# A recurrent mixer on one core: the heads' values projected token-major in four units, centred by row means, and three convolution units moved between the heads

## The chip, the cores and the metric

The kernel runs on one core of one Trainium2 chip. The metric is the time of one execution on the device in microseconds (us). The core has five engines that run side by side and meet through semaphores: TensorE (PE; its weight loads are shown as PEld), VectorE (DVE), ScalarE (ACT), GpSimd (POOL) and SyncE (SP), which here only issues DMAs.

## The reference

A network over 512 tokens of width 1024, all in float32. It starts with two layers (`DEPTH = 2`) that have a mixer between two feed-forward parts. Only these two mixers are touched; what follows them (attention, memory, a linear recurrence) is not:

```python
p = rmsnorm(x, mix_norm) @ w_in          # 512 + 768 + 2048 columns
y_a = gmlp_mixer(p[:, :512])             # gelu, group layer norm, 128x128 token mixing
y_b = shortconv_mixer(p[:, 512:1280])    # bg, cg, xin: bg * conv3(cg * xin)
y_c = retention_mixer(p[:, 1280:])       # 4 heads of 128: q, k, v, gate
x = x + concat(y_a, y_b, y_c) @ w_out

# retention, per head and chunk of 128 tokens
q, k = rotary(q), rotary(k) * 128 ** -0.5
scores = (q @ k.T) * decay
inner = scores @ v
kv = (k * zeta).T @ v                    # the state that a chunk hands on
state = state * gamma + kv
ret = inner + (q @ previous_state) * xi
ret = layernorm_over_the_head(ret) * gn
y_c = silu(g) * ret
```

The layer norm takes the mean over the 128 values of a head away. Since `ret` is linear in `v`, the kernel takes the mean out of `v` at once and only divides by the root of the variance at the end.

## The kernel before, in words

Activations lie with features on partitions and the 512 tokens along the columns. A weight matrix comes as a stream of units of 128 x 1024 float32 (eight blocks of 128 x 128, one for each 128 input features). There are 588 units and four slots. For each unit SP loads `raw`, ACT rounds it to fp32r (`whi`, in `split_hi`, called as `ahead(key)` two units ahead), POOL subtracts to get the rest (`wlo`), and PE makes 24 matmuls of 512 columns: `whi` by the high and by the low part of the activations, `wlo` by the high part. `project` does a whole unit; `high` and `low` do its first 16 and its last 8, so that something can stand between them. Four PSUM banks go round (`next_bank`); 4 to 7 are claimed by name. The order on every engine is written out by hand.

The mixer (`mixer1`, once in each engine's program) goes through 26 units. Units 0 to 3 feed the gated part (gelu, group means and variances). Then come four heads of four units each:

* unit 4+4h gives v with features on partitions; DVE multiplies it by the token scale R into `vT`. After two more units, `vturn` multiplies each 128-token block of `vT` by the matrix `centring` (identity less 1/128): that turns it to tokens on partitions and takes the head mean away in one go. ACT copies it to `vtok`.
* units 5+4h and 6+4h give k and q; DVE rotates each with four operations (`rotate`), into `kr` and `qr`.
* unit 7+4h gives the gate. Between its `high` and `low` PE turns `kr` (`kturn`), and after it come `kv1`, `score1`, the products with the states, and `inner`.
* PE takes the variance of head h-1 (`head_variance`) after the first unit of head h. DVE then does `finish_head(h-1)`: a reciprocal, two products and `split`, which writes the high and the low part of y tile 4+h-1.

DVE also has the two `gate_norm` (a reciprocal and a product each) at the ends of heads 0 and 1. After the heads PE turns the gated values, runs unit 20, `head_variance(3)`, the token mixing (`gmix`), then units 21 to 25 for the two convolution tiles, and then `output`. DVE goes through `conv_gate(0)`, `gmlp(0)`, `gmlp(1)`, `conv(0)`, `finish_head(3)`, `conv_gate(1)`, `conv(1)`. `output` multiplies by w_out with the y tiles in the order

```python
Y_ORDER = (4, 5, 6, 0, 1, 7, 2, 3)
for m in range(X_EARLY):     # 3 output tiles, the first six y tiles of each
    part((kind, a, m), banks[m][:, :], pairs, range(0, 6), True, False, arrive if m == 0 else None)
```

so that in the first output tile PE waits for each y tile just before it uses it: tiles 4, 5, 6 (heads 0 to 2), 0 and 1 (the gated part), 7 (head 3), and, after 54 matmuls, 2 and 3 (the convolutions).

Of the kernel before, what the change touches and what calls it, by code (L numbers as in the profile page):

```python
# [6 lines left out]
F32 = mybir.dt.float32  # L7
# [6 lines left out]
P = 128  # L14
# [30 lines left out]

F_STAGE = (0, 2, 3, 5, 8, 11)
# [31 lines left out]
def unit_order():  # L78
# [8 lines left out]
    def mixer1(l):  # L87
        out.extend(("m1", l, n) for n in range(26))
        out.extend(("o1", l, m) for m in range(KD))
# [29 lines left out]
def low_part(u):  # L119
# [5 lines left out]
    "m1_vector": "ga ws rot_table gelu_lo csq_lo centred centring z0 vinv vn hinv ret_n ret_g y1h y1 rot_c rot_s rot_in rope vT gg sm "  # L125
                 "sg ret qx state rsq_lo gbias gm cg cg2 z cv cvR cy",
    "m1_scalar": "gelu gelu_hi csq csq_hi vroot hroot vtok ktok silu1 rsq rsq_hi vtg",
    "m1_tensor": "mean var hvar vturn kturn kv1 score1 inner gturn gmix",
# [40 lines left out]
class Memory:  # L169
# [51 lines left out]
    def mixer1_tiles(self, l):  # L221
        return self.scoped(f"m1{l}", [
            ("yh", KD * SEQ, F32R), ("yl", KD * SEQ, F32R), ("ct", SEQ, F32), ("sn", SEQ, F32),
            ("dk", 2 * C_HEADS * P + C_HEADS, F32), ("below_qx", 5 * P - C_HEADS, F32), ("qx", 3 * P, F32), ("ws", 4 * P, F32), ("bs", 2 * P, F32), ("kr", SEQ, F32), ("qr", SEQ, F32),
            ("t1", SEQ, F32), ("vT", SEQ, F32), ("vtok", SEQ, F32), ("sm", SEQ, F32),
            ("ktok", 3 * P, F32), ("state", 3 * P, F32), ("ret", SEQ, F32),
            ("rsq", SEQ, F32), ("inv", SEQ, F32), ("sg", SEQ, F32), ("centring", P, F32), ("ga", SEQ, F32),
# [96 lines left out]
def tensor_program(pe, S, M):  # L324
# [156 lines left out]
    def mixer1(l):  # L481
# [35 lines left out]
        for h in range(C_HEADS):  # L517
            b = next_bank("vT", l, h)
            high(("m1", l, 4 + 4 * h), b[:, :])
            if h == 0:  # L520
                gate_variances()
            low(("m1", l, 4 + 4 * h), b[:, :])
            if h:
                head_variance(h - 1)
            project(("m1", l, 5 + 4 * h), next_bank("rot_in", l, h, 0)[:, :])
            project(("m1", l, 6 + 4 * h), next_bank("rot_in", l, h, 1)[:, :])
            b4 = claim(4, "vtok", l, h)
            pe.wait_ge(*S.at("vT", l, h))
# [13 lines left out]
            pe.wait_ge(*S.at("vtok", l, h))  # L542
# [2129 lines left out]
```

## Time and profile before

| | |
|---|---|
| median of 3 runs | 3239.8 us (3239.62 to 3239.84) |
| the profiled execution | 3240.1 us, its span in the trace 3238.8 us |
| PE busy | 3227.0 us, 14914 matmuls |
| DVE, POOL, ACT busy | 1592.7, 1331.1 and 1090.2 us |
| granted clock of TensorE | full over the span |
| HBM read | 316 MB, 98 GB/s over the span |

The span is what the trace covers; the execution's own time is a little longer. An engine's busy time is the union of its instructions. A line of the profile can be that of a helper: L363, L364 and L367 are `unit`, L378 and L379 `high`, L385 `low`.

### The profile page before, as it was taken

What the parts mean: (1) busy time and instruction counts of PE and PEld (TensorE: products, weight loads), DVE (VectorE), ACT (ScalarE), POOL (GpSimd) and SP (SyncE); (2) the same over time, 40 slices, a digit from 0 to 9 for tenths busy, and PEclk for the clock granted to TensorE, in tenths of its full rate; (3) what the DMA queues carried; (4) which work ended last, traced back from release to release, by engine and by line L of the source; (5) the groups of instructions that cost most, each with busy time, mean ns of one, the idle gap of its engine ahead of it and who ended that gap; (6) DMA issues with size and microseconds to landing.
All of it is one profiled execution on the core that took longest, in us unless ns stands there. A gap on an engine that the chain in (4) does not pass through costs nothing.

```text
span 3238.8 us, 36579 instructions
## 1 busy us (share of the span) xinstructions
PE 3227.0 (100%) x14914; PEld 2678.1 (83%) x14914; DVE 1592.7 (49%) x1845; ACT 1090.2 (34%) x1449; POOL 1331.1 (41%) x551
## 2 busy tenths in 40 slices
PE   9999999999999999999999999999999999999999
PEld 7888888888888888888888877888888888988887
DVE  6441277554234531676544267545444486454421
ACT  4222332322232222433222345543222475432222
POOL 4444433544444445334444432224444213154443
PEclk9999999999999999999999999999999999999999
DMA  4223322322232223322323322323222223232222
GB/s 151 98 98 104 116 72 81 108 98 98 98 111 93 99 95 104 106 82 91 104 92 101 104 92 66 124 92 104 98 98 101 98 92 136 92 104 98 98 94 82
DMA packets 92182, 321.57 MB, mean 99 GB/s; under 512 B 10480, under 2 KB 12912, under 8 KB 92016
## 3 DMA queue, kind: packets, MB, share of 16 engines
q1 hardware_dynamic: 86624, 311.54, 28.9%
q10 hardware_dynamic: 5392, 7.69, 0.7%
q8 instruction: 119, 1.95, 0.3%
q14 instruction: 47, 0.39, 0.0%
HBM read 316.05 MB, written 2.10 MB: 98 GB/s over the span
## 4 chain that ended last, share of the span: by engine, by line
PE 99%; DVE 1%; DMA 0%; ACT 0%; issue 0%; ACTq 0%; DVEq 0%
PE bank L363 20%; PE bank L367 20%; PE bank L364 20%; PE bank L378 9%; PE bank L385 9%; PE bank L379 9%; PE bank L348 1%; PE bank L349 1%; PE bank L352 1%; PE bank L642 1%; PE bank L662 1%; PE bank L767 0%; PE bank L762 0%; PE bank L761 0%; PE bank L394 0%; PE bank L395 0%
## 5 line engine op out<-in xcount | busy, mean ns | idle before, releaser
L2488 POOL TENSOR_TENSOR wlo<-raw,whi 128x1024 fp32r<-128x1024 f32 x535 | 1326.5, 2489 | 1886.1 <-ACT whi L950 1885.6
L950 ACT ACTIVATE whi<-raw 128x1024 fp32r<-128x1024 f32 x588 | 611.8, 1052 | 594.6 <-PE bank L385 382.0
L363 PE MATMUL bank<-gxh,whi 128*128 128x512 f32 x1552 | 606.2, 391 | 0.0
L364 PE MATMUL bank<-gxl,whi 128*128 128x512 f32 x1552 | 604.1, 389 | 0.0
L378 PE MATMUL bank<-gxh,whi 128*128 128x512 f32 x1296 | 507.0, 391 | 2.2 <-ACT whi L950 2.2
L379 PE MATMUL bank<-gxl,whi 128*128 128x512 f32 x1296 | 504.4, 389 | 0.0
L363 PE MATMUL bank<-f_hh,whi 128*128 128x512 f32 x1056 | 410.8, 389 | 0.0
L364 PE MATMUL bank<-f_hl,whi 128*128 128x512 f32 x1056 | 410.8, 389 | 0.0
L367 PE MATMUL bank<-gxh,wlo 128*128 128x512 f32 x1552 | 383.6, 389 | 0.0
L1760 DVE TENSOR_TENSOR f_u<-bank,R 128x512 f32<-128x512 f32 x132 | 91.2, 691 | 583.0 <-PE bank L385 583.0
L1705 DVE SCALAR_TENSOR_TENSOR x<-bank,x 128x512 f32<-128x512 f32 x96 | 66.4, 692 | 565.1 <-PE bank L367 539.2
L363 PEld LDWEIGHTS bank<-gxh,whi 128*128 128x128 f32 x1552 | 291.3, 188 | 61.8 <-issue 0.7
L367 PEld LDWEIGHTS bank<-gxh,wlo 128*128 128x128 f32 x1552 | 291.2, 188 | 60.9 <-DVE wlo L1666 0.4
L364 PEld LDWEIGHTS bank<-gxl,whi 128*128 128x128 f32 x1552 | 291.3, 188 | 60.7 <-issue 0.7
L385 PE MATMUL bank<-gxh,wlo 128*128 128x512 f32 x1296 | 322.8, 391 | 0.0
L1765 DVE TENSOR_SCALAR f_hh<-f_u 128x512 fp32r<-128x512 f32 x132 | 312.1, 2364 | 4.5
L1024 ACT ACTIVATE f_s<-f_a 128x512 f32<-128x512 f32 x132 | 83.4, 632 | 638.6 <-DVE f_a L1756 638.6
L378 PEld LDWEIGHTS bank<-gxh,whi 128*128 128x128 f32 x1296 | 243.3, 188 | 54.6 <-issue 2.3
L385 PEld LDWEIGHTS bank<-gxh,wlo 128*128 128x128 f32 x1296 | 242.5, 188 | 51.1 <-issue 1.0
L379 PEld LDWEIGHTS bank<-gxl,whi 128*128 128x128 f32 x1296 | 243.3, 188 | 49.6
L367 PE MATMUL bank<-f_hh,wlo 128*128 128x512 f32 x1056 | 262.7, 389 | 0.0
L988 ACT ACTIVATE sq<-x 128x512 f32<-128x512 f32 x96 | 60.6, 632 | 573.2 <-DVE x L1705 573.2
(406 smaller groups left out, 3564.6 us busy)
## 6 DMA issues: line engine op xcount, KB each, us to landing
raw<-stream SPq DMA_DIRECT2D x588, 512.0 KB, 3.3
xa_mem<-memT ACTq DMA_DIRECT2D x2, 1024.0 KB, 6.1
m_dk<-decay ACTq DMA_DIRECT2D x2, 514.0 KB, 4.4
x<-xT ACTq DMA_DIRECT2D x4, 256.0 KB, 5.7
x<-xT SPq DMA_DIRECT2D x4, 256.0 KB, 6.9
outT<-x ACTq DMA_DIRECT2D x4, 256.0 KB, 2.2
outT<-x SPq DMA_DIRECT2D x4, 256.0 KB, 2.6
m_ct<-cos ACTq DMA_DIRECT2D x2, 256.0 KB, 2.7
```

Of the source, the lines that this page charges most:

```text
L363: pe.matmul(out, seq(hi, k, P), h, start=first and k == 0, stop=False)
L364: pe.matmul(out, seq(hi, k, P), l, start=False, stop=False)
L367: mm = pe.matmul(out, seq(lo, k, P), h, start=False, stop=last and k == len(pairs) - 1)
L378: pe.matmul(out, seq(hi, k, P), gx[k][0], start=k == 0, stop=False)
L379: pe.matmul(out, seq(hi, k, P), gx[k][1], start=False, stop=False)
L385: mm = pe.matmul(out, seq(lo, k, P), gx[k][0], start=False, stop=k == KD - 1)
L950: act.activation(M.whi[r][:, :], M.raw[r][:, :], ACT.Copy).then_inc(*S.tick("hi", u))
L1024: act.activation(T["s"][:, :], T["a"][:, :], ACT.Silu).then_inc(*S.tick("silu", f, m))
L1705: dve.scalar_tensor_tensor(seq(M.x, m), at_bank("xs", i, m)[:, :], scale, seq(M.x, m), ALU.mult, ALU.add).then_inc(*S.tick("xs", i, m))
L1760: dve.tensor_tensor(T["u"][:, :], at_bank("u", f, m)[:, :], M.R[:, :], ALU.mult).then_inc(*S.tick("u", f, m))
L1765: dve.tensor_scalar(seq(T["hh"], m), T["u"][:, :], 1.0, None, ALU.mult).then_inc(*S.tick("hh", f, m))
L2488: pool.tensor_tensor(M.wlo[r][:, :], M.raw[r][:, :], M.whi[r][:, :].bitcast(F32), ALU.subtract).then_inc(*S.tick("lo", u))
```

## The change

* The values of all four heads come first, in four units of their own, ("m1v", l, 0) to ("m1v", l, 3). A unit holds two blocks of input features (k) by all 512 value columns. The 128-token blocks of the activations are now the stationary operand and the weight's 512 columns the moving one, so the result has tokens on partitions: bank n holds tokens 128n to 128n+127 of all four heads. Four ring banks are open over all four units.
* `norm` stands in the second of these units. Behind it `column_sums` makes the per-token sums of squares as a column (4 float32 matmuls of one column); ACT takes the root, DVE the reciprocal.
* For each bank DVE sums each head's 128 columns (`reduce_sum`) and makes the bias, minus mean times token scale; ACT writes `vtok` with four activations of 128 x 128 with scale and bias. The products of the heads read their block of `vtok`.
* Gone: the units 4, 8, 12 and 16 (their weights are in the new units), the DVE product into `vT`, the matrix `centring`, `vturn` and its 4 float32 matmuls a head, and the ACT copy a head.
* Units 20, 21 and 22 (the first convolution tile) move from behind the heads to the place where v stood in heads 1, 2 and 3. On DVE `conv_gate(0)`, `conv_sum(0)` and `conv_out(0)` stand there, ahead of `finish_head(h-1)`.
* The tables (`ct`, `sn`, `ws`) are scaled on DVE ahead of the row means; `gate_norm(0)` goes between the two rotations of head 0, `gate_norm(1)` to the end of head 0.
* Behind the heads PE has unit 23, `head_variance(3)`, `gmix`, units 24 and 25, `output`. DVE has `gmlp(0)`, `gmlp(1)`, `finish_head(3)`, `conv_gate(1)`, `conv_sum(1)`, `conv_out(1)`.

The core of the diff (`conv_sum` and `conv_out` are the two parts of the old `conv`, unchanged):

```diff
+M1_UNITS = (0, 1, 2, 3, 5, 6, 7, 20, 9, 10, 11, 21, 13, 14, 15, 22, 17, 18, 19, 23, 24, 25)
...
 tensor_program
+        def column_sums():
+            b = claim(6, "col_root", l)
+            pe.wait_ge(*S.at("acc", i - 1, KD - 1))
+            for n in range(NB):
+                mm = pe.matmul(b[:, n:n + 1], seq(M.acc, n, P), M.ones[:, 0:1], start=n == 0, stop=n == NB - 1)
+            mm.then_inc(*S.tick("colsum", l))
+
+        def token_values():
+            banks = []
+            for j in range(4):
+                u = U["m1v", l, j]
+                hi, lo = M.whi[u % SLOTS], M.wlo[u % SLOTS]
+                pe.wait_ge(*S.at("hi", u))
+                for blocks in ((0, 1), (2, 3)) if j == 3 else (range(NB),):
+                    for n in blocks:
+                        if j == 0:
+                            banks.append(next_bank("vtok", l, n))
+                        for k in (2 * j, 2 * j + 1):
+                            if n == 0:
+                                pe.wait_ge(*S.at("gx", i - 1, k))
+                            h, lw = (seq(t, k)[:, n * P:(n + 1) * P] for t in (M.gxh, M.gxl))
+                            pe.matmul(banks[n][:, :], h, seq(hi, k % 2), start=k == 0, stop=False)
+                            pe.matmul(banks[n][:, :], lw, seq(hi, k % 2), start=False, stop=False)
+                    if j == 1:
+                        norm(i)
+                        column_sums()
+                    pe.wait_ge(*S.at(*low_part(u)))
+                    for n in blocks:
+                        for k in (2 * j, 2 * j + 1):
+                            mm = pe.matmul(banks[n][:, :], seq(M.gxh, k)[:, n * P:(n + 1) * P], seq(lo, k % 2),
+                                           start=False, stop=k == KD - 1)
+                        if j == 3 and n < NB - 1:
+                            mm.then_inc(*S.tick("vdone", l, n))
+                mm.then_inc(*S.tick("used", u))
...
         for h in range(C_HEADS):
-            b = next_bank("vT", l, h)
-            high(("m1", l, 4 + 4 * h), b[:, :])
+            if h:
+                project(("m1", l, 19 + h), next_bank(("cg", "z", "cy")[h - 1], l, 0)[:, :])
+                head_variance(h - 1)
+            b = next_bank("rot_in", l, h, 0)
+            high(("m1", l, 5 + 4 * h), b[:, :])
             if h == 0:
                 gate_variances()
-            low(("m1", l, 4 + 4 * h), b[:, :])
-            if h:
-                head_variance(h - 1)
-            project(("m1", l, 5 + 4 * h), next_bank("rot_in", l, h, 0)[:, :])
+            low(("m1", l, 5 + 4 * h), b[:, :])
             project(("m1", l, 6 + 4 * h), next_bank("rot_in", l, h, 1)[:, :])
-            b4 = claim(4, "vtok", l, h)
-            pe.wait_ge(*S.at("vT", l, h))
-            pe.wait_ge(*S.at("centring", l))
-            for n in range(NB):
-                mm = pe.matmul(seq(b4, n, P), seq(T["vT"], n, P), T["centring"][:, :], start=True, stop=True)
-            mm.then_inc(*S.tick("vturn", l, h))
...
-        project(("m1", l, 20), next_bank("cg", l, 0)[:, :])
+        project(("m1", l, 23), next_bank("cg", l, 1)[:, :])
         head_variance(C_HEADS - 1)
...
-        for j in range(2):
-            if j:
-                project(("m1", l, 23), next_bank("cg", l, 1)[:, :])
-            project(("m1", l, 21 + 3 * j), next_bank("z", l, j)[:, :])
-            project(("m1", l, 22 + 3 * j), next_bank("cy", l, j)[:, :])
+        project(("m1", l, 24), next_bank("z", l, 1)[:, :])
+        project(("m1", l, 25), next_bank("cy", l, 1)[:, :])
...
 scalar_program
+        for n in range(NB):
+            act.wait_ge(*S.at("vbias", l, n))
+            for h in range(C_HEADS):
+                act.activation(seq(T["vtok"], n * C_HEADS + h, P), seq(bank[BANK["vtok", l, n]], h, P), ACT.Identity,
+                               bias=T["vcols"][:, 6 * NB + n * C_HEADS + h:6 * NB + n * C_HEADS + h + 1],
+                               scale=T["vcols"][:, NB + n:NB + n + 1]).then_inc(*S.tick("vtok", l, n))
...
             if h:
-                ahead(("m1", l, 4 + 4 * h))
+                ahead(("m1", l, 19 + h))
                 head_root(h - 1)
-            ahead(("m1", l, 5 + 4 * h))
+                ahead(("m1", l, 5 + 4 * h))
             ahead(("m1", l, 6 + 4 * h))
-            act.wait_ge(*S.at("vturn", l, h))
-            if h:
-                act.wait_ge(*S.at("inner", l, h - 1))
-            act.activation(T["vtok"][:, :], bank[4][:, :], ACT.Copy).then_inc(*S.tick("vtok", l, h))
             ahead(("m1", l, 7 + 4 * h))
...
 vector_program
+        for n in range(NB):
+            sums, bias = (T["vcols"][:, c + n * C_HEADS:c + (n + 1) * C_HEADS] for c in (2 * NB, 6 * NB))
+            dve.wait_ge(*(S.at("vdone", l, n) if n < NB - 1 else used("m1v", l, 3)))
+            dve.reduce_sum(sums, at_bank("vtok", l, n)[:, :].rearrange("p (h d) -> p h d", d=P), AX.X).then_inc(
+                *S.tick("vsum", l, n))
+            dve.wait_ge(*S.at("vsum", l, n))
+            dve.tensor_scalar(bias, sums, T["vcols"][:, NB + n:NB + n + 1], -1.0 / P, ALU.mult, ALU.mult).then_inc(
+                *S.tick("vbias", l, n))
...
         for h in range(C_HEADS):
-            dve.wait_ge(*used("m1", l, 4 + 4 * h))
             if h:
-                dve.wait_ge(*S.at("vturn", l, h - 1))
-            dve.tensor_tensor(T["vT"][:, :], at_bank("vT", l, h)[:, :], M.R[:, :], ALU.mult).then_inc(*S.tick("vT", l, h))
-            if h:
+                (conv_gate, conv_sum, conv_out)[h - 1](0)
                 finish_head(h - 1)
             rotate(h, 0, T["kr"])
+            if h == 0:
+                gate_norm(0)
             rotate(h, 1, T["qr"])
...
-            if h < 2:
-                gate_norm(h)
+            if h == 0:
+                gate_norm(1)
...
-        conv_gate(0)
         gmlp(0)
         gmlp(1)
-        conv(0)
         finish_head(C_HEADS - 1)
         conv_gate(1)
-        conv(1)
+        conv_sum(1)
+        conv_out(1)
```

## Rows read from the trace of the kernel before

**Rows 1.** The page: its span and first part (busy us, share, instructions)

```profile
span 3238.8 us, 36579 instructions
...
PE 3227.0 (100%) x14914; PEld 2678.1 (83%) x14914; DVE 1592.7 (49%) x1845; ACT 1090.2 (34%) x1449; POOL 1331.1 (41%) x551
```

**Rows 2.** Waits of PE: us in total, times, longest us

```profile
PE bank L378 <- ACT whi L950: 2.2, 1, 2.2
...
PE bank L458 <- DVE R L2461: 0.4, 1, 0.4
```

**Rows 3.** Timeline of PE, vturn of head 0: start us, us, engine, line

```profile
410.27 1.06 PE L531 MATMUL bank<-m_centring,m_vT 128*128 128x128 f32 x8
...
411.09 0.48 PE L378 MATMUL bank<-gxh,whi 128*128 128x512 f32 x1
...
411.40 0.39 PE L379 MATMUL bank<-gxl,whi 128*128 128x512 f32 x1
```

**Rows 4.** Timeline of PE, one-column float32 sums of another block

```profile
2037.02 0.95 PE L737 MATMUL bank<-ones,acc 128*128 128x1 f32 x8
2037.83 0.49 PE L363 MATMUL bank<-gxh,whi 128*128 128x512 f32 x1
```

**Rows 5.** Timeline of PE, from gmix to output, first mixer

```profile
508.72 2.57 PE L577 MATMUL bank<-m_ws,m_vtg 128*64 128x128 f32 x32
...
538.57 0.39 PE L348 MATMUL bank<-m_yh,whi 128*128 128x512 f32 x1
```

**Rows 6.** Timeline of DVE behind the heads, first mixer

```profile
511.06 2.32 DVE L1904 TENSOR_TENSOR m_ga<-m_ga,m_u 128x512 f32<-128x512 f32 x1
...
521.53 0.68 DVE L1921 TENSOR_TENSOR m_z<-bank,m_cg 128x512 f32<-128x512 f32 x1
...
522.77 1.54 DVE L1926 SCALAR_TENSOR_TENSOR m_cg<-m_z,lcol,m_cg 128x512 f32<-128x512 f32 x2
...
529.01 3.34 DVE L1827 RECIPROCAL m_inv<-m_inv 128x512 f32<-128x512 f32 x1
...
534.30 0.69 DVE L1777 TENSOR_TENSOR m_yl<-m_ret,m_yh 128x512 fp32r<-128x512 f32 x1
...
539.16 3.76 DVE L1926 SCALAR_TENSOR_TENSOR m_cg<-m_z,lcol,m_cg 128x512 f32<-128x512 f32 x2
```

**Rows 7.** Timeline of POOL, first mixer

```profile
428.24 4.76 POOL L2488 TENSOR_TENSOR wlo<-raw,whi 128x1024 fp32r<-128x1024 f32 x2 [1.79 <-ACT whi L950]
...
523.65 2.91 POOL L2488 TENSOR_TENSOR wlo<-raw,whi 128x1024 fp32r<-128x1024 f32 x1 [3.04 <-ACT whi L950]
...
539.97 2.40 POOL L2488 TENSOR_TENSOR wlo<-raw,whi 128x1024 fp32r<-128x1024 f32 x1 [2.72 <-ACT whi L950]
```

**Rows 8.** Timeline of PE in head 1: first matmul and kturn

```profile
420.42 0.48 PE L378 MATMUL bank<-gxh,whi 128*128 128x512 f32 x1
...
441.88 0.49 PE L538 MATMUL bank<-ident,m_kr 128*128 128x128 f32 x3
```

**Rows 9.** Timeline of DVE in head 1, and vT of head 3

```profile
427.71 0.68 DVE L1855 TENSOR_TENSOR m_vT<-bank,R 128x512 f32<-128x512 f32 x1
...
431.69 1.86 DVE L1829 TENSOR_TENSOR m_ret<-m_ret,m_inv 128x512 f32<-128x512 f32 x1
...
437.54 0.69 DVE L1848 TENSOR_TENSOR m_kr<-m_kr,m_t 128x512 f32<-128x512 f32 x1
...
480.40 0.69 DVE L1855 TENSOR_TENSOR m_vT<-bank,R 128x512 f32<-128x512 f32 x1 [2.44 <-PE bank L385]
```

**Rows 10.** Windows at the end: PE, PEld, DVE, ACT, POOL busy, PEclk, DMA

```profile
3231.50:3232.00 0.50, 0.40 (x1) 0.00 (x0) 0.50 (x2) 0.06 (x1) 0.00 (x0) 1.00 0.00 0
...
3236.00:3236.40 0.40, 0.00 (x0) 0.00 (x0) 0.00 (x0) 0.00 (x0) 0.00 (x0) 0.88 1.00 374
```

**Rows 11.** Groups by form: a reduction on DVE, the vtok copy on ACT

```profile
L2207 DVE TENSOR_REDUCE xa_mx<-bank 128x2 f32<-128x512 f32 x16 | 10.9, 683 | 5.1 <-PE bank L786 5.1
...
L1071 ACT ACTIVATE m_vtok<-bank 128x512 f32<-128x512 f32 x4 | 2.4, 600 | 38.6 <-PE bank L531 38.6
```

More of the change, by code:

```diff
@@ L87, in mixer1 @@
     def mixer1(l):
-        out.extend(("m1", l, n) for n in range(26))
+        out.extend(("m1v", l, j) for j in range(4))
+        out.extend(("m1", l, n) for n in M1_UNITS)
         out.extend(("o1", l, m) for m in range(KD))
@@ L558, in mixer1 @@
             for n in range(NB):
-                mm = pe.matmul(seq(b4, n, P), seq(T["vtok"], n, P), seq(T["sm"], n, P), start=False, stop=n == NB - 1)
+                mm = pe.matmul(seq(b4, n, P), seq(T["vtok"], n * C_HEADS + h, P), seq(T["sm"], n, P), start=False, stop=n == NB - 1)
             mm.then_inc(*S.tick("inner", l, h))
@@ L1032, in mixer1 @@
             act.dma_start(t[:, :], src).then_inc(*S.tick("tables", l, by=16))
[L1033 removed]
+        ahead(("m1v", l, 0))
+        ahead(("m1v", l, 1))
+        root(i)
+        act.wait_ge(*S.at("colsum", l))
+        act.activation(T["vcols"][:, 0:NB], bank[6][:, 0:NB], ACT.Sqrt, bias=EPS, scale=1.0 / D).then_inc(
+            *S.tick("col_root", l))
+        ahead(("m1v", l, 2))
+        ahead(("m1v", l, 3))
+        ahead(("m1", l, 0))
+        for n in range(NB):
[4 more added lines that the diff above has]
+                               scale=T["vcols"][:, NB + n:NB + n + 1]).then_inc(*S.tick("vtok", l, n))
         ahead(("m1", l, 1))
[L1035 removed]
         for j in range(4):
@@ L1515, in bank_plan @@
         residual(F_STAGE[2 * l])
+        for n in range(NB):
+            out["vtok", l, n] = ring.next()
         for j in range(4):
@@ L1518, in bank_plan @@
         for h in range(C_HEADS):
-            out["vT", l, h], out["rot_in", l, h, 0], out["rot_in", l, h, 1], out["gg", l, h] = ring.many(4)
-        for j in range(2):
-            out["cg", l, j], out["z", l, j], out["cy", l, j] = ring.many(3)
+            if h:
+                out[("cg", "z", "cy")[h - 1], l, 0] = ring.next()
+            out["rot_in", l, h, 0], out["rot_in", l, h, 1], out["gg", l, h] = ring.many(3)
+        out["cg", l, 1], out["z", l, 1], out["cy", l, 1] = ring.many(3)
         residual(M1_STAGE[l])
@@ L1848, in rotate, with gmlp @@
             dve.tensor_tensor(out[:, :], out[:, :], T["t1"][:, :], ALU.add).then_inc(*S.tick("rope", l, h, e))
+        def gmlp(j):
+            dve.wait_ge(*S.at("gmix", l, j))
+            bias = seq(T["bs"], j, P)[:, None, :].to_broadcast([P, NB, P])
+            dve.wait_ge(*S.at("silu1", l, C_HEADS - 1))
+            if j:
+                dve.wait_ge(*S.at("y1", l, j - 1))
+            dve.tensor_tensor(T["ga"][:, :].rearrange("p (n t) -> p n t", n=NB),
+                              bank[4 + j][:, :].rearrange("p (n t) -> p n t", n=NB), bias, ALU.add).then_inc(
+                *S.tick("gbias", l, j))
+            dve.wait_ge(*S.at("gbias", l, j))
+            dve.wait_ge(*S.at("gelu", l, 2 + j))
+            dve.tensor_tensor(T["ga"][:, :], T["ga"][:, :], seq(T["u"], j), ALU.mult).then_inc(*S.tick("gm", l, j))
+            dve.wait_ge(*S.at("gm", l, j))
+            split(T["ga"][:, :], j)
@@ L2563, in stream @@
             [10 + 12 + h for h in range(4)]
-        order = [2, 3, 0, 1]
-        order += [head[n][h] for h in range(4) for n in range(4)]
-        order += [6, 8, 4, 7, 9, 5]
+        of = [2, 3, 0, 1]
+        of += [head[n][h] for h in range(4) for n in range(4)]
+        of += [6, 8, 4, 7, 9, 5]
+        order = [of[n] for n in M1_UNITS]
+        v = i["w_in"][l][:, 18 * P:22 * P].reshape(4, 2, P, SEQ).transpose(0, 2, 1, 3).reshape(4, P, UNIT)
         wo = i["w_out"][l].reshape(KD, P, D)[list(Y_ORDER)].reshape(D, D)
-        out += [w[order], m_tiles(wo)]
+        out += [v, w[order], m_tiles(wo)]
         out += [pairs(i["ffn2_w_gate"][l], i["ffn2_w_up"][l]), tail_units(i["ffn2_w_down"][l])]
```

121 lines of the change are left out of this document (53 added, 68 removed).

## The prediction

> **What bounds the kernel now.** I read the page first: TensorE is busy for 3227.0 of 3238.8 us, and no other engine for half of the span [rows 1]. Then the waits of PE: three rows, the first and last of which are shown, with 3.7 us in all, and none of them in the two mixers [rows 2]. So the time is the sum of what PE issues. Less PE work shortens it one for one, and work taken off DVE, ACT or POOL gives nothing by itself. What can cost time is an order in which DVE, so far always early, comes late for PE. So I read the timelines of the mixer and laid the new order over them. The second mixer repeats the first; the rows shown are the first's.
>
> **What PE no longer does.** In `vturn` four float32 matmuls show as eight instructions. The first starts at 410.27 and the next matmul of the gate unit at 411.09, so they take 0.82 us; that next matmul itself takes 0.31 to the one behind it, where the usual pace is 0.23 [rows 3]. Without `vturn` a head is 0.90 us shorter; with 4 heads in 2 mixers this is **-7.2 us**. The number of units and of 512-column matmuls stays as it is: four new units of 24 stand for four old ones. Their operands change places, but each still loads 128 columns and streams 512. I take their pace as unchanged.
>
> **What PE does in addition.** `column_sums` has four float32 matmuls of one column. The same thing stands elsewhere in the kernel: 2037.02 to 2037.83, 0.81 us [rows 4], plus the same 0.09 at the change back. This is 0.9 us a mixer, **+1.8 us**.
>
> **The front, up to the gated units.** The four new banks go back to the ring for units 0 to 3, so the first `vtok` bank has to be read by the end of the fourth value unit. Its last matmul has 14 others behind it in that unit, 3.2 us. In that time DVE sums it (0.68 for 128x512, and I add 0.25 for the start and 0.1 for the bias), and ACT writes four blocks of 128x128. The nearest row is 0.60 us for 128x512 [rows 11], so four take 0.6 (by columns) to 2.4 (by instructions). I take 0.9, since most of the 0.60 goes with the columns. The sum is 1.9, and 0.6 more if the small DVE operation finds POOL at work, which I expect, since the third weight split of the stage comes then. That leaves 0.6 us: cost 0. With 2.4 for ACT and a whole POOL operation of 2.4 in front, it would be 2.6 us a mixer. The other edits here are free in the same way. The scaled tables fill a stretch in which DVE waits for the value units, and `gate_norm(0)` fits between the rotations of head 0: by my count its q is ready 0.7 us before the scores want it.
>
> **Behind the heads: the main cost.** `gmix` starts at 508.72 and takes 2.57; `output` starts at 538.57, five units later. That gives 27.28 us for 120 matmuls, 0.227 each, 5.45 a unit [rows 5]. Now only two units stand there, so `output` starts at 522.2 on the same scale. Ten matmuls later, at 524.5, it wants y tile 7, which `finish_head(3)` writes. On DVE, `gmlp(0)` and `gmlp(1)` take until 521.53, as in the trace [rows 6]: they start when `gmix` ends, and the weight splits of ACT and POOL beside them go by the same finished units in either kernel. `finish_head(3)` comes next: its reciprocal from 521.53 takes 3.34, and from its start to the end of its last operation the trace has 534.30 + 0.69 - 529.01 = 5.98 us [rows 6]. That alone gives 527.5. But POOL starts an operation at 523.65 [rows 7], and so it will again, as the split of the unit after next goes by the end of the second unit behind `gmix`. A DVE operation with both inputs in SBUF then waits for it: 511.06 shows 2.32 us for one that takes 0.69 free [rows 6]. `ret_n` asks at 524.9 and POOL is done at 526.0, so it ends at 526.6 and tile 7 is ready at 528.5. PE stands for 4.0 us, **+8.1 us** over both mixers. In the old order three more units, 16.4 us, covered this. Tile 3, the last one, is 6.8 us of DVE work behind, at 535.3, and wanted 54 matmuls and more after the stall, at 538.9, so there is no second wait. With no POOL operation in the way at all (5.9 us less in `gmlp`, 1.1 in `ret_n`) tile 7 would come at 521.5 and the wait would be 0: these are the ends, 0 and 8.1.
>
> The Trainium skill ("SBUF — State Buffer", section "Who interferes with whom") says that a DVE instruction with two SBUF inputs contends with a GpSimd instruction that reads SBUF, and that "Whoever issues first gets the shared pair for the whole instruction". The row at 511.06 agrees: 2.32 us in place of 0.69. By a reading in which they only share bandwidth, the wait behind the heads would be shorter.
>
> **The heads.** In head 1 the first matmul is at 420.42 and `kturn` at 441.88 [rows 8]. Without `vturn` PE wants the rotated k at 440.98. Before, it was ready at 438.23, 4.68 us after `ret_n` had ended at 433.55 [rows 9].
> Head 1: `conv_gate(0)` starts where `vT` did, 427.71 [rows 9]. Its second product asks at 428.4 and meets the POOL pair that starts at 428.24 with 2.38 each [rows 7]. It gets in after the first, 430.6, and is done at 431.2; POOL's second goes to 433.6. The reciprocal runs to 434.5. The next split used to wait on ACT behind `vturn`. Now it goes by unit 9, so POOL is at it from 433.6 to 436.0, `ret_n` ends at 436.6 and k is ready at 441.3: 0.35 us late, and 0.15 more because `qx` then holds up the states. In sum 0.5.
> Head 2, on the same scale: `conv_sum(0)` starts when its unit is done, at 426.2 (as `vT` does in head 3 [rows 9]). Its second sum would start at 428.20, POOL's pair at 428.24. Who wins is open. In the trace, with 0.11 us between them (523.54 and 523.65) DVE won, with 0.04 (539.93 and 539.97) POOL did and the pair of sums took 3.76 us in place of 1.54 [rows 6, 7]. If DVE wins, the products and the head's end fall behind two POOL operations and k is 0.8 late; if POOL wins, 1.85. With 0.15 for the states, 1.0 or 2.0; I take 1.5.
> Head 3: `conv_out(0)` is 1.8 us long, and k comes 0.5 us in time: 0.
> This makes 2.0 us a mixer, **+4.0 us**, with the ends 0 (POOL never in the way) and 5.0 (head 2 at 2.0, head 1 at 0.5) and a little more if head 3 slips.
>
> **Sum.** -7.2 + 1.8 + 0 + 8.1 + 4.0 = +6.7 us. The profiled execution took 3240.1 us, of which the span is 3238.8; the median shown is 0.3 lower. So 3240.1 + 6.7 - 0.3 = **3246.5 us**.
>
> **Rivals.**
> 1. *Not slower: the end of head 3 is in time.* This is one mechanism: POOL keeps out of `gmlp` and `ret_n`. It decides from 4.0 us earlier on. For it: with no POOL there, DVE needs 11.2 us from `gmlp(0)` on, and the cover is 14.2. Against it: the same blocks stand in both mixers of the trace. It gives 3246.5 - 8.1 = 3238.4.
> 2. *The heads hide everything.* DVE reaches `kturn` in time in all heads. For it: before, k was 3.6 us early in each. Against: my count of POOL operations. 3246.5 - 4.0 = 3242.5. With 1 and 2 together 3234.4, all of PE's saving; that would still be within 0.2%.
> 3. *The clock falls in the wait.* Full clock was still granted at 3232 us, where PE's last work ended, and it fell (from 2.4 towards 1.2 GHz) within 3236.0 to 3236.4, some 4.4 us later [rows 10]. My wait is 4.0 us long, just short of it. If it falls, matmuls at half the clock for about as long as the fall took, an estimate, cost 2.2 us each time: 3248.7 or 3250.9. The Trainium skill ("TensorE: Matmul & The Clock Gate", section "Why this matters for your kernels") warns that a long idle gap between bursts of matmuls takes the clock to its lower level. The rows at the end agree that it falls, and no run so far shows one inside the kernel.
> 4. *The front stalls*: up to 2.6 us a mixer, 3247 to 3252.
>
> **Chances.** My forecast with both outcomes of head 2 (3245.5 to 3247.5): 0.45. Rival 1: 0.1. Rival 2: 0.15, and both together 0.05. Rival 3: 0.15. Rival 4: 0.1. The range is 3240.5 to 3250.5: it leaves out rival 1 and the pair, and the far ends of 3 and 4. What a measurement of this kernel can tell from no change is about 0.2%, 6.5 us. The forecast sits on that bound (3246.3). Half of its own case, rivals 3 and 4 and a little of the rest lie above: slower 0.49, same 0.46. Faster by 6.5 us would need more than the 5.4 us that PE saves net, so it gets 0.05 for something I have not seen.
>
> **What would show it.** No L531 and about 64 fewer PE instructions for it, 16 more with one column. In the waits of PE's weight loads: two of some 4 us on `m_yl` at the first `output` unit, and four between 0.3 and 2 us at `kturn` in heads 1 and 2. The `vtok` copies should end before the fourth value unit does. If PE shows no wait at tile 7, my order of DVE and POOL behind the heads is wrong; if there are waits at unit 0 or in head 0, the front is.

## The result: 3251.9 us, 0.4% slower

| | before | after |
|---|---|---|
| median of 6 runs | 3239.82 us (3239.62 to 3240.08) | 3251.88 us (3251.15 to 3253.97) |
| ratio, 95% interval | | 1.0039 (1.0028 to 1.0049) |
| profiled execution, its span | 3240.1, 3238.8 us | 3251.4, 3248.8 us |

I forecast 3246.5 us, range 3240.5 to 3250.5. The direction was the likelier one of the forecast, the size is 5.4 us above it and outside the range. In the page of the changed kernel PE's busy time has not moved from [rows 1], and the span is 10.0 us longer:

```profile
span 3248.8 us, 36499 instructions
PE 3227.0 (99%) x14866; PEld 2675.3 (82%) x14866; DVE 1592.9 (49%) x1853; ACT 1098.0 (34%) x1475; POOL 1332.4 (41%) x551
```

48 instructions are gone, as forecast (64 of `vturn` less, 16 of the column sums more). The version without waits further down has the same matmuls and shows PE busy for 3222.5 us, so they were worth 4.5 us of busy time; that 3227.0 stands here again means that the remaining matmuls took as much longer, 3.4 of it at a lower clock (below). The waits of PE, to be read beside [rows 2], say where PE stood still (us in total, times, longest):

```profile
PE bank L351 <- DVE m_yl L1820: 8.0, 2, 4.1
PE bank L570 <- DVE m_kr L1897: 2.3, 2, 1.7
PE bank L381 <- ACT whi L979: 1.4, 1, 1.4
...
PE bank L582 <- DVE m_qr L1897: 0.4, 2, 0.2
```

L351 is the first tile of `output`, L570 `kturn`, L582 the scores. The timeline of PE at the first `output` unit of the first mixer, and a mixer later, answers to [rows 5]:

```profile
538.91 0.39 PE L352 MATMUL bank<-m_yl,whi 128*128 128x512 f32 x1
543.14 0.50 PE L351 MATMUL bank<-m_yh,whi 128*128 128x512 f32 x1 [3.85 <-DVE m_yl L1820]
...
1476.61 0.39 PE L352 MATMUL bank<-m_yl,whi 128*128 128x512 f32 x1
1481.12 0.50 PE L351 MATMUL bank<-m_yh,whi 128*128 128x512 f32 x1 [4.12 <-DVE m_yl L1820]
...
1484.55 0.63 PE L351 MATMUL bank<-m_yh,whi 128*128 128x512 f32 x1
1484.98 0.63 PE L352 MATMUL bank<-m_yl,whi 128*128 128x512 f32 x1
```

The tenth matmul starts at 538.91, the eleventh was due at 539.13 and comes at 543.14: 4.0 us late, and 4.3 in the second mixer. DVE behind the heads, beside [rows 6]:

```profile
524.96 0.69 DVE L1905 TENSOR_TENSOR m_ga<-bank,m_bs 128x512 f32<-128x512 f32 x1 [5.26 <-PE bank L609]
525.68 2.32 DVE L1910 TENSOR_TENSOR m_ga<-m_ga,m_u 128x512 f32<-128x512 f32 x1
...
536.15 3.35 DVE L1876 RECIPROCAL m_inv<-m_inv 128x512 f32<-128x512 f32 x1
539.53 1.64 DVE L1878 TENSOR_TENSOR m_ret<-m_ret,m_inv 128x512 f32<-128x512 f32 x1
...
542.39 0.69 DVE L1820 TENSOR_TENSOR m_yl<-m_ret,m_yh 128x512 fp32r<-128x512 f32 x1
543.00 0.68 DVE L1920 TENSOR_TENSOR m_cg<-bank,R 128x512 f32<-128x512 f32 x1
```

Tile 7 is ready when its `yl` ends, at 543.1, and PE goes on at 543.14. The last two PE rows above show what the forecast left to a rival: they start 0.43 us apart, and [rows 5] had 0.227. The windows of the first mixer (us, PE busy, then the granted clock, DMA share, GB/s):

```profile
542.00:543.00 1.00, 0.00 (x0) 1.00 0.88 315
543.00:544.00 1.00, 0.86 (x3) 0.82 0.35 139
544.00:545.00 1.00, 1.00 (x3) 0.50 0.00 0
...
546.00:547.00 1.00, 1.00 (x4) 0.50 0.00 0
547.00:548.00 1.00, 1.00 (x5) 0.97 0.07 16
```

PE's last matmul ahead of the wait began at 538.91. The clock still stood at 1.00 through all of the wait, fell to 0.50 (1.2 of 2.4 GHz) only between 543 and 544, when PE was back at work, and came back between 547 and 548. Summed over the windows that is 0.18 + 3 x 0.50 + 0.03 = 1.7 us of work lost; the second mixer has the same, 1.7. In the second mixer the clock fell 1.2 us after PE's return (0.66 in the window from 1482 to 1483). So the wait costs 4.0 or 4.3 and 1.7 more behind it.

The Trainium skill ("TensorE: Matmul & The Clock Gate", section "Why this matters for your kernels") says to leave no long idle gap between bursts of matmuls. These windows agree, and show the fall after the gap.

In the heads the forecast's steps can be checked one by one. DVE and POOL at the `conv_sum` of head 2 in both mixers, and at the rotation of head 0 (DVE first):

```profile
424.03 2.90 DVE L1897 TENSOR_TENSOR m_kr<-m_kr,m_t 128x512 f32<-128x512 f32 x1
...
433.05 0.69 DVE L1897 TENSOR_TENSOR m_qr<-m_qr,m_t 128x512 f32<-128x512 f32 x1
...
470.18 1.54 DVE L1932 SCALAR_TENSOR_TENSOR m_cg<-m_z,lcol,m_cg 128x512 f32<-128x512 f32 x2
...
1406.80 3.78 DVE L1932 SCALAR_TENSOR_TENSOR m_cg<-m_z,lcol,m_cg 128x512 f32<-128x512 f32 x2
```

```profile
421.62 4.76 POOL L2537 TENSOR_TENSOR wlo<-raw,whi 128x1024 fp32r<-128x1024 f32 x2 [7.78 <-ACT whi L979]
...
471.02 8.13 POOL L2537 TENSOR_TENSOR wlo<-raw,whi 128x1024 fp32r<-128x1024 f32 x3 [1.81 <-ACT whi L979]
...
1407.63 8.03 POOL L2537 TENSOR_TENSOR wlo<-raw,whi 128x1024 fp32r<-128x1024 f32 x3 [1.79 <-ACT whi L979]
```

Head 2 is the race that the forecast left open. In the first mixer DVE's second sum was at work when POOL started at 471.02, and the pair took 1.54 us; in the second POOL started at 1407.63, DVE's second sum had to wait for it, and the pair took 3.78. The same program goes one way in one mixer and the other way in the other. In head 0 POOL has two operations from 421.62 to 426.38, not one. The second starts at 423.98 in the trace, 0.05 us before the last addition for k, which asks at 424.03 and is done only at 426.9. With `gate_norm(0)` next, q is ready at 433.7, a little after the scores want it. The waits of the weight loads, second mixer (the first has 1.5 at L570 and 4.3 at L351):

```profile
PEld bank L351 <- DVE m_yl L1820: 4.5, 1, 4.5
PEld bank L570 <- issue: 2.5, 2, 2.1
...
PEld bank L582 <- issue: 0.4, 1, 0.4
...
PEld bank L381 <- ACT m_vtok L1074: 0.2, 1, 0.2
```

L381 is unit 0, which waits for the copies of the values. An idle time of the weight loads is a few tenths longer than what PE itself loses by it, so the account goes by the starts of PE's matmuls.

**The account.** I take a mixer from the start of the last matmul of the feed-forward part ahead of it to the start of the last `wlo` matmul of `output`. Before, the two took 212.3 and 212.4 us. In the version without waits further down ("spread and tail") they take 209.7 each: this is PE's own saving, 5.3 in sum. Here they take 216.9 and 218.3. Of this the output has 4.0 + 4.3 = 8.3 of waits and 3.4 of clock. The heads, from `kturn` of head 0 to `gmix`, are 1.4 and 2.6 longer than in that version, 4.0 in sum: at `kturn` PE loses 0.2 and 0.8 us in heads 1 and 2 of the first mixer, 0.2 and 1.9 in the second, and 0.4 a mixer at the scores of head 0. The first gated unit has under 0.1. At the start of the kernel the first unit begins at 7.85, before at 8.39, so 0.5 less. The sum is -5.3 + 8.3 + 3.4 + 4.0 - 0.5 = +9.9, the span shows +10.0. The profiled execution has 2.6 us of its time outside the span; the five others, with spans of 3249.9 to 3252.5, have 1.3 to 1.5, as before.

### The profile page after: what moved, and what is told of

It is laid out like the page before. It is cut to its first block, busy times and chain, and to the rows that moved or that the text cites. A ratio compares the mean times of both kernels' runs of the same rounds, so it can differ in the third digit from the quotient of the medians.

```text
span 3248.8 us, 36499 instructions
## 1 busy us (share of the span) xinstructions
PE 3227.0 (99%) x14866; PEld 2675.3 (82%) x14866; DVE 1592.9 (49%) x1853; ACT 1098.0 (34%) x1475; POOL 1332.4 (41%) x551
## 4 chain that ended last, share of the span: by engine, by line
PE 94%; DVE 5%; issue 0%; ACT 0%; DMA 0%; ACTq 0%; DVEq 0%
PE bank L366 19%; PE bank L370 19%; PE bank L367 19%; PE bank L381 9%; PE bank L388 9%; PE bank L382 9%; PE bank L355 1%; PE bank L351 1%; PE bank L352 1%; DVE m_inv L1876 1%; PE bank L671 1%; PE bank L691 1%; PE bank L796 0%; PE bank L790 0%; PE bank L791 0%; PE bank L534 0%
## 5 line engine op out<-in xcount | busy, mean ns | idle before, releaser
L366 PE MATMUL bank<-gxh,whi 128*128 128x512 f32 x1472 | 575.5, 391 | 0.0
L367 PE MATMUL bank<-gxl,whi 128*128 128x512 f32 x1472 | 572.9, 389 | 0.0
L381 PE MATMUL bank<-gxh,whi 128*128 128x512 f32 x1312 | 512.2, 390 | 1.4 <-ACT whi L979 1.4
L382 PE MATMUL bank<-gxl,whi 128*128 128x512 f32 x1312 | 510.6, 389 | 0.0
L370 PE MATMUL bank<-gxh,wlo 128*128 128x512 f32 x1472 | 363.7, 389 | 0.0
L388 PE MATMUL bank<-gxh,wlo 128*128 128x512 f32 x1312 | 326.5, 391 | 0.0
L366 PEld LDWEIGHTS bank<-gxh,whi 128*128 128x128 f32 x1472 | 276.4, 188 | 58.2 <-issue 0.7
L370 PEld LDWEIGHTS bank<-gxh,wlo 128*128 128x128 f32 x1472 | 276.3, 188 | 57.9 <-DVE wlo L1709 0.4
L367 PEld LDWEIGHTS bank<-gxl,whi 128*128 128x128 f32 x1472 | 276.4, 188 | 57.3 <-issue 0.7
L381 PEld LDWEIGHTS bank<-gxh,whi 128*128 128x128 f32 x1312 | 246.3, 188 | 55.3 <-DVE gxl L1778 2.3
L382 PEld LDWEIGHTS bank<-gxl,whi 128*128 128x128 f32 x1312 | 246.3, 188 | 50.7
L388 PEld LDWEIGHTS bank<-gxh,wlo 128*128 128x128 f32 x1312 | 245.5, 188 | 51.4 <-issue 1.0
```

The source lines that it names most:

```text
L366: pe.matmul(out, seq(hi, k, P), h, start=first and k == 0, stop=False)
L367: pe.matmul(out, seq(hi, k, P), l, start=False, stop=False)
L370: mm = pe.matmul(out, seq(lo, k, P), h, start=False, stop=last and k == len(pairs) - 1)
L381: pe.matmul(out, seq(hi, k, P), gx[k][0], start=k == 0, stop=False)
L382: pe.matmul(out, seq(hi, k, P), gx[k][1], start=False, stop=False)
L388: mm = pe.matmul(out, seq(lo, k, P), gx[k][0], start=False, stop=k == KD - 1)
```

## Experiments

The waits at the output and in the heads, and the low clock after them, are what has to be told apart. All medians are against 3239.7 to 3239.8 of the kernel before on the same chip, whose runs lie within 0.7 us but for one.

| version | median (runs) | ratio, 95% | wait at output | waits at kturn, scores | clock lost in the mixers |
|---|---|---|---|---|---|
| after | 3251.9 (6) | 1.0039 (1.0028-1.0049) | 8.8 | 4.0, 0.8 | 3.4 |
| y order | 3247.0 (11) | 1.0021 (1.0012-1.0030) | 6.5 | 4.0, 0.8 | 1.7 |
| filled | 3248.1 (11) | 1.0024 (1.0016-1.0033) | 1.5 | 5.0, 0.8 | 0 |
| half filled | 3247.1 (1) | | 5.2 | 4.0, 0.8 | 0 |
| split late | 3255.4 (5) | 1.0049 (1.0036-1.0062) | 8.8 | 4.2, 3.6 | 8.5 |
| spread | 3242.4 (11) | 1.0008 (0.9999-1.0017) | 6.5 | 0, 0 | 3.4 |
| spread and tail | 3235.4 (11) | 0.9986 (0.9977-0.9995) | 0 | 0, 0 | 0 |
| tail alone | 3238.5 (11) | 0.9997 (0.9988-1.0006) | 0 | 4.0, 0.8 | 0 |
| convolution alone | 3252.1 (5) | 1.0038 (1.0024-1.0052) | 8.6 | 0, 0 | 3.4 |
| values alone | 3254.2 (5) | 1.0044 (1.0030-1.0057) | 0 | 18.4, 0 | 1.7 |

The waits are idle time of the weight loads in the profiled execution, the rounded rows of both mixers added, which is a few tenths a wait more than PE itself loses. Half filled has a single run. For split late the second number of the heads is a wait at the products with the states. Clock lost is the sum of (1 - granted clock) over the windows of the mixers.

**Another order of the y tiles.** The wait for tile 7 goes if the tile is not among the first six.

```diff
-Y_ORDER = (4, 5, 6, 0, 1, 7, 2, 3)
+Y_ORDER = (4, 5, 6, 2, 0, 1, 7, 3)
```

> The changed kernel with the y tiles in the order 4, 5, 6, 2, 0, 1, 7, 3, so that head 3's tile is wanted after 54 matmuls and not after 10. Theory: the wait of 4.0 and 4.3 us at that tile in the two mixers goes, and with it both falls of the granted clock (some 1.7 us each), as they follow from that wait. From 3251.9 us that is -8.3 - 3.4, so 3240 us, with 1.00 granted throughout. Rival a: the clock falls for another reason (the short waits in the heads), then only -8.3: 3243.5 us. Rival b: a wait of another kind takes its place, at tile 0 or tile 1, which are now wanted one tile later: 3246 us or more.

It gave 3247.0, not 3240. The wait for tile 7 is gone, and another stands at the start of the second output tile, eight matmuls behind where tile 7 was wanted. Weight loads of PE, and DVE beside them:

```profile
544.07 0.29 PEld L351 LDWEIGHTS bank<-m_yh,whi 128*128 128x128 f32 x1 [3.09 <-DVE m_cg L1920]
```

```profile
543.33 0.68 DVE L1920 TENSOR_TENSOR m_cg<-bank,R 128x512 f32<-128x512 f32 x1
```

The second output tile takes the PSUM bank that held `cg(1)`, and DVE empties it only behind `finish_head(3)`, at 544.0. In the changed kernel this wait is hidden behind the other: `cg(1)` is read 0.6 us after tile 7, and PE, which had stood for 4.0 us, does not reach the second tile before. My forecast had not looked at that bank at all. The clock fell at the end of the wait of 3.1 us in the first mixer (0.92 in the window from 543 to 544) and not with that of 3.4 in the second.

**Matmuls in place of the wait.** To price the clock alone, 16 matmuls of 512 columns go into a spare bank right before PE waits for tile 7, their result unused; half filled has 8 of them. Nothing else changes.

```diff
+            if fill is not None and k == 5:
+                for _ in range(16):
+                    pe.matmul(fill[:, :], M.rounded_ones[:, :], seq(M.gxh, 0), start=True, stop=True)
             if arrive:
                 pe.wait_ge(*S.at(*arrive[k]))
```

> The changed kernel with 16 matmuls of 512 columns into a spare bank (3.6 us of work, results unused) right before PE waits for head 3's tile. They end before the tile is there. Theory: the wait for the tile is as long as before, but TensorE does not idle in it and the clock does not fall, so only the 3.4 us of the clock go: 3248.5 us, PEclk 1.00 in the two stretches. Rival: the clock has nothing to do with the idle time in the wait; then nothing changes, 3251.9 us, and PEclk shows 0.50 again some 4 us behind.

> The changed kernel with 8 matmuls of 512 columns into a spare bank ahead of y tile 7 (twice as many closed the wait wholly and the clock stayed at 1.00). About 2.2 us of the wait is left in each mixer. If a fall of the clock needs an idle stretch of over 3 us, none is lost here (the start of the kernel has a wait of 2.2 us without one). If a stretch of 2 us is enough, as in the second mixer's head 2 of the late-split version, both falls stay, 1.7 us each.

3248.1: the kernel with 32 matmuls more is 3.8 us faster than the changed one, and its clock stays at 1.00 in every window of the mixers. Windows of PE (us, PE busy, clock, DMA share, GB/s), filled:

```profile
542.00:544.00 2.00, 2.00 (x10) 1.00 0.52 156
544.00:546.00 2.00, 1.86 (x8) 1.00 0.30 115
```

The medians alone don't price the clock to a tenth, since the profiled spans differ by 1.9 only (3248.8 and 3246.9): here head 2 went the costly way in both mixers, 1.0 more. The stretch of `output` does: from the start of its first matmul to that of its last it takes 47.5 and 47.8 us, against 49.1 and 49.3 in the changed kernel. That is 3.1 less, of the 3.4 that the windows put down to the clock. With 8 a mixer (half filled) it is the same, 47.5 and 47.7. PE still stands for 2.0 and 2.3 us, and again no window lies below 1.00. Timeline of PE, half filled:

```profile
540.29 2.03 PE L351 MATMUL bank<-gxh,rounded_ones 128*128 128x512 f32 x8
544.34 0.50 PE L354 MATMUL bank<-m_yh,whi 128*128 128x512 f32 x1 [2.02 <-DVE m_yl L1824]
```

So a wait of about 2 us costs itself; one of about 4 costs more each time it was seen; around 3 (2.7 to 3.0 in PE's own rows) it goes either way: one of two in the y order version, two of two in spread (below), one of six in values alone.

**The next weight split behind `kturn`'s copy.** This keeps POOL out of `finish_head` by starting the split for the gate unit later.

```diff
-            ahead(("m1", l, 7 + 4 * h))
             act.wait_ge(*S.at("tables", l))
...
                 *S.tick("ktok", l, h))
+            ahead(("m1", l, 7 + 4 * h))
             act.wait_ge(*S.at("gg", l, h))
```

> The changed kernel with ScalarE's split for the unit two ahead, in each head, moved back behind the copy of k (ktok), about where vturn used to hold it. Theory: POOL's operation for that unit then no longer stands in the way of DVE's products in finish_head, k comes in time for kturn in head 1 (0.45 us in each mixer) and in head 2 when DVE wins the race for its second sum (1.05), and the scores of head 0 no longer wait (0.37). The head 2 in which POOL wins keeps most of its 2.1. Sum -2.7 to -4.8 us: 3247 to 3249 us. Rival: DVE simply has too much to do in front of kturn, whatever POOL does; then the waits at kturn stay and the time stays at 3252 us.

It came out some 7 us above that. Head 0 and head 1 have no wait any more, as expected. Head 2 has two, in both mixers. DVE there, and POOL:

```profile
469.69 3.78 DVE L1932 SCALAR_TENSOR_TENSOR m_cg<-m_z,lcol,m_cg 128x512 f32<-128x512 f32 x2
...
487.74 2.58 DVE L1955 TENSOR_TENSOR m_qx<-m_qr,m_dk 128x384 f32<-128x384 f32 x1
```

```profile
470.52 5.20 POOL L2537 TENSOR_TENSOR wlo<-raw,whi 128x1024 fp32r<-128x1024 f32 x2 [1.80 <-ACT whi L979]
...
487.33 2.58 POOL L2537 TENSOR_TENSOR wlo<-raw,whi 128x1024 fp32r<-128x1024 f32 x1 [11.61 <-ACT whi L979]
```

POOL won the race at the sums both times, and the split that was moved away from `finish_head` now meets `qx`, which takes 2.58 us and makes PE wait 1.8 more at the products with the states. The clock fell behind one of the two pairs of waits (1.7 us). Behind the waits of 4 us at the output, as long as in the changed kernel, it fell for twice as long. Windows of this version (PE, PEld, DVE, ACT, POOL busy, then the clock):

```profile
544.00:545.00 1.00, 0.00 (x0) 0.00 (x0) 0.93 (x3) 0.00 (x0) 0.00 (x0) 0.55 0.83 172
...
549.00:550.00 1.00, 1.00 (x4) 0.81 (x3) 0.93 (x3) 0.00 (x0) 0.00 (x0) 0.50 0.00 0
550.00:551.00 1.00, 1.00 (x4) 0.74 (x4) 0.90 (x2) 0.00 (x0) 0.00 (x0) 0.54 0.07 16
```

PE's wait goes from 541.7 to 545.7 here; the clock falls in its midst, and stays down for 6.8 us, 3.4 us of clock in each mixer. No run shows why it came earlier and lasted longer here. Moving POOL's work only moves the collision; what it needs is an order on DVE in which nothing urgent stands there.

**The convolution's DVE work spread.** With the new y order and the late split, the gate norms go back to the ends of heads 0 and 1, and the long part of each convolution step (`conv_gate_too` is the second product with R, `conv_taps` the three taps, `conv_scale` their product with R) goes behind `qx` and, for the last, behind `rsq_lo`, where PE does not wait for DVE:

```diff
-                (conv_gate, conv_sum, conv_out)[h - 1](0)
+                (conv_gate_in, conv_sum_in, conv_out)[h - 1](0)
                 finish_head(h - 1)
             rotate(h, 0, T["kr"])
-            if h == 0:
-                gate_norm(0)
             rotate(h, 1, T["qr"])
...
+            if h == 1:
+                conv_gate_too(0)
+            if h == 2:
+                conv_taps(0)
...
-            if h == 0:
-                gate_norm(1)
+            if h < 2:
+                gate_norm(h)
+            if h == 2:
+                conv_scale(0)
```

> A version meant to be better than both: the y order of e1, the late split of e3, the two gate_norm back at the ends of heads 0 and 1, and of the first convolution only the product that empties the PSUM bank in front of finish_head; its second gate product, its three taps and its last scaling go to places where DVE waits anyway (behind qx, and behind the square of head 2). Theory: every wait of PE that the change brought goes, and what is left is the work removed less the column sums: -7.2 + 1.8 = -5.4 us against the kernel before, 3234.5 us. Rival: some of these operations meet POOL there and hold up the states or the next head; then 3236 to 3240 us, with waits at L582, L588 or L570 in the list.

All waits of the heads are gone. 3242.4 and not 3234.5, because the wait for the bank of `cg(1)` was not in the expectation, nor the 3.4 us of clock that come with it. Against the kernel before this is no clear difference (0.9999 to 1.0017). The waits of the weight loads, first mixer, name it:

```profile
PEld bank L351 <- DVE m_cg L1920: 3.1, 1, 3.1
```

**A tail order that frees the bank first.** DVE idles behind the last head until `gmix` is done. There the two gate products of the second half fit, and `z`, the first product of its sum, goes ahead of `finish_head(3)`; `conv_sum` here is without the taps and the product with R, which `conv_taps` has:

```diff
-        gmlp(0)
-        gmlp(1)
-        finish_head(C_HEADS - 1)
         conv_gate(1)
-        conv_sum(1)
+        gmlp(0)
+        gmlp(1)
+        conv_sum(1)
+        finish_head(C_HEADS - 1)
+        conv_taps(1)
         conv_out(1)
```

> On top of the spread version (242.4 us over 3000 there): behind the heads DVE does the gate products of the second convolution half before the gate unit's own work, and its sum before the end of head 3. My theory: the waits left there (3.1 and 3.4 us at the second output tile, on the bank of the second conv gate) and the low clock that follows them (3.8 us of lost clock) are all that separates that version from a mixer with no stall. So no wait of over 0.5 us in the mixers, clock 1.00, and 3242.4 - 6.5 - about 1.9 = 3234 us (3233.5 to 3235.5). Rival a: DVE needs about 24 us for all of it and the cover is about 25, so its last tile comes late: waits of about 1 us on the last y tile, 3236 to 3238. Rival b: the low clock has nothing to do with the waits: clock still falls, about 3236.

> The changed kernel with the new order of y tiles and of DVE's work behind the heads, heads untouched. My theory (a sum of independent terms): it removes the 8.3 us of waits at the output and the lost clock that follows (3.4 us), and leaves the waits of the heads (4.1 us at kturn, 0.7 at the scores of head 0). 3251.9 - 8.3 - 3.4 = 3240.2 us (3239 to 3241.5), no wait at the output. Rival: the waits of the heads also let the clock fall, then 3242 to 3244.

With the heads spread it gave 3235.4 for 3234 (3233.5 to 3235.5), inside the range and 1.4 above its middle. With the heads as they were it gave 3238.5 for 3240.2 (3239 to 3241.5), 0.5 below the range. On the spread version: 3235.4, its span 3233.2, 5.6 us under [rows 1]. This is PE's saving, 5.3 in the two mixers, and 0.35 at the start of the kernel: no wait on PE in the mixers, clock 1.00. DVE of this version behind the heads, and PE in the two mixers by windows:

```profile
521.76 0.69 DVE L1920 TENSOR_TENSOR m_cg<-bank,R 128x512 f32<-128x512 f32 x1 [3.30 <-PE bank L370]
...
535.53 3.34 DVE L1876 RECIPROCAL m_inv<-m_inv 128x512 f32<-128x512 f32 x1
...
545.90 0.69 DVE L1820 TENSOR_TENSOR m_yl<-m_cg,m_yh 128x512 fp32r<-128x512 f32 x1
```

```profile
365.00:560.00 195.00, 194.55 (x943) 1.00 0.27 87
1300.00:1510.00 210.00, 209.55 (x1009) 1.00 0.28 90
```

`cg(1)` is read at 521.76 instead of 543.00, in time that DVE had free. On the changed kernel with its heads as they were, the tail order and the y order alone give 3238.5, which is within the interval of the kernel before (0.9988 to 1.0006) and 13.4 us less than the changed kernel. The profiled spans (3248.8 and 3237.3) differ by 11.5, and the traces account for that: 8.3 of waits and 3.4 of clock. The other 1.9 lie between the changed kernel's profiled execution and its other runs. The waits of the heads, 2.1 us at most, let no clock fall. The two tail versions differ in their heads only, and their spans by 4.1: that is what the heads cost. The race in head 2 went the other way round here, costly in the first mixer and cheap in the second.

**Each half of the change alone.** The kernel before with only the three convolution units between the heads:

> The kernel before with one part of the change alone: three convolution units stand between the heads instead of behind them, with their DVE work; the values keep their place and the turn of the values stays. My theory: the missing cover behind the heads is the cost, so PE waits about 4 us for y tile 7 in each mixer and loses about 1.7 us of clock after each: 3239.8 + 8.3 + 3.4 = 3251.5 us (3249 to 3253), with waits at kturn below 1 us since each head keeps its own PE work. Rival: the costs come from the token-major values and their centring; then this version is at 3240 to 3242 with no wait over 1 us at the output.

And the changed kernel with all six convolution units back behind the heads, in the old order:

```diff
-M1_UNITS = (0, 1, 2, 3, 5, 6, 7, 20, 9, 10, 11, 21, 13, 14, 15, 22, 17, 18, 19, 23, 24, 25)
+M1_UNITS = (0, 1, 2, 3, 5, 6, 7, 9, 10, 11, 13, 14, 15, 17, 18, 19, 20, 21, 22, 23, 24, 25)
...
-        gmlp(0)
-        gmlp(1)
-        finish_head(C_HEADS - 1)
-        conv_gate(1)
+        conv_gate(0)
+        gmlp(0)
+        gmlp(1)
+        conv_sum(0)
+        conv_out(0)
+        finish_head(C_HEADS - 1)
+        conv_gate(1)
```

> The changed kernel without the move of the convolution: all six of its units stand behind the heads as before, with their DVE work in the old order; only the values are token-major and centred by row means. My theory: behind the heads there is no wait. In the heads, PE wants the rotated k one unit (5.45 us) and the 0.90 us of the turn earlier than before, and DVE is done only 0.7 us earlier (no vT product). Before, k was 3.6 us early in heads 1 and 2, so it is 2.0 us late now in each; head 3 has no gate norm ahead of it on DVE and is in time. 3239.8 - 7.2 + 1.8 + 4 x 2.0 = 3242.4 us (3240 to 3247 with POOL's operations falling otherwise). Rival a: the values alone give all of the saving: 3234.5 us, no wait at kturn. Rival b: the scores and the products behind them slip too, by a unit in each head: over 3250.

The convolution alone costs 12.4 us: the waits of the output (PE, both mixers, 7.7) and 3.4 us of clock, nothing in the heads. The values alone cost 14.5, where I expected 2.7. Waits of PE, first mixer (the second has the same row):

```profile
PE bank L569 <- DVE m_kr L1897: 8.0, 3, 2.7
```

Three heads wait, not two, and longer. Head 3 shows why, on ACT, DVE and PE:

```profile
491.18 0.60 ACT L1103 ACTIVATE m_inv<-bank 128x512 f32<-128x512 f32 x1 [1.38 <-PE bank L553]
```

```profile
491.81 3.35 DVE L1876 RECIPROCAL m_inv<-m_inv 128x512 f32<-128x512 f32 x1 [3.54 <-ACT m_inv L1103]
...
502.09 0.69 DVE L1897 TENSOR_TENSOR m_kr<-m_kr,m_t 128x512 f32<-128x512 f32 x1
```

```profile
490.76 0.39 PE L553 MATMUL bank<-sum_lo,rounded_ones 128*128 128x512 f32 x1
...
502.93 0.52 PE L569 MATMUL bank<-ident,m_kr 128*128 128x128 f32 x3 [2.67 <-DVE m_kr L1897]
```

DVE was idle for 3.54 us before the reciprocal, so the gate norms, on which my expectation turned, are not the reason here. From the end of PE's variance product, 491.15, to the rotated k, 502.78, there are 11.6 us of root, reciprocal, head and rotation. PE has only one whole unit (5.45) and 16 matmuls (3.63) in between, 9.1 us. In the kernel before, a unit and the turn more stood there, 15.4 us; in the changed one 14.5. So the values' change needs a unit put between the heads, and the unit taken for it is missed behind them: each half alone is a loss, and the halves together cost less than their sum (12.1 against 26.9).

## Why the prediction was wrong

- **PE's saving, -7.2 and +1.8: right.** With every wait gone the mixers are 5.3 us shorter.
- **The output, +8.1: right.** Measured 8.3. DVE's order, its meeting with POOL at `gmlp` (2.32 again) and `ret_n` (1.64) went as laid over. "Tile 3 ... so there is no second wait" was true of tile 3 and blind to a bank: a wait of 3.1 us stood hidden behind the first, and came out as soon as that was removed.
- **The step that failed: "My wait is 4.0 us long, just short of it."** I had read in [rows 10] that the clock fell some 4.4 us after PE's last work, and took 4.4 us for the length of idling that it needs. That was one fall, read as a rule, and the windows after show that it is none. Behind the waits of 4.0 and 4.3 the low clock came 4.3 and 5.3 us after the end of PE's last matmul, with PE already working again; in other versions it came with waits of about 3 us, and with the late split in the midst of the wait, as early as 2.2 us. This rival, to which I gave 0.15, was the case, in both mixers. Its cost here was 1.7 each time and not 2.2. It is 3.4 of the 5.4 us that were missing; the filled version, with its `output` 3.1 shorter at a clock of 1.00, shows that they follow from the idling.
- **The heads, +4.0: the mechanism right, the sum by luck.** PE lost 4.0 in all, but 0.8 of it is in head 0, where I had nothing. At `kturn` it lost 0.2 in head 1 in both mixers (forecast 0.35), nothing in head 3, and in head 2, which was to be 0.8 or 1.85 by the race, 0.8 in one mixer and 1.9 in the other.
- **Head 0, 0: mis-sized, measured 0.8.** "`gate_norm(0)` fits ... q is ready 0.7 us before the scores want it" had one POOL operation in the way; there are two (4.76 us), k's last addition met the second and took 2.90.
- **The front, 0: right, under 0.1 for PE** (0.4 by the idle time of its weight loads). The small bias operation did find POOL at work (0.56 in place of 0.23), and the copies take 0.36 each when grouped (5.69 for 16), 1.4 for a bank, between my 0.9 and the bound of 2.4.
- **The range.** I didn't have the start of the kernel, 0.5 less. Its top of 3250.5 left out "the far ends of 3 and 4". The clock in both mixers was 3250.9 by my own sum, with nothing else going wrong. Of the 5.4 us, the span explains 3.3 (+10.0 for +6.7). The profiled execution has 1.3 more outside its span than the one before, and the median lies 0.5 above it, where I had put it 0.3 below: this makes the other 2.1, and nothing here shows their cause. That the spans of the other five runs go up to 3252.5 and the clock of some down to 0.998 would fit the race and the clock, but there is no trace of them.

## What to carry to other kernels

When PE is the bound and work is moved out of a stretch, count the cover of every engine's chain behind that stretch, and then look what is second: for each wait found, ask which bank or tile would be next if it were gone. A wait of a few microseconds on TensorE has to be priced with the low clock behind it, and cheap filler matmuls tell the two apart. Where DVE has a fixed chain between two points of PE, the PE work between those points is a budget; put what PE doesn't wait for outside of it, into DVE's idle time. Here that turned +12.1 into -4.3 us.

## What was not expected of the hardware

- The granted clock can fall after the fact: at 1.00 for a whole wait of 4.0 us, at 0.50 for 3.4 us once PE was back, then at 1.00 again; or in the midst of such a wait and for 6.8 us. Waits of 2.3 us and less showed no fall by themselves (two of 2.1 and 1.8, close together, had one behind them in one mixer of the late split and none in the other), waits near 3 us sometimes (4 of 10), waits of about 4 us each time (6 of 6: changed kernel, split late, convolution alone).
- A DVE operation of 128 x 4 elements with SBUF operands is held up by POOL as well: 0.56 us for 0.23.
- The race of DVE and POOL is decided within hundredths of a microsecond (DVE's second sum at 470.97 and POOL at 471.02: 1.54 us for the pair; 1407.59 and 1407.63: 3.78), in the same program once each way, and is worth 1.1 us of PE's time.
